# The second attention of a two-layer trunk: a bank of PSUM and a quarter of the probabilities' room for each step of the first tile

## What is computed

```python
SEQ, D_MODEL, CHUNK, Q_BLOCK = 256, 1024, 64, 128
C_HEADS, C_NOPE, C_ROPE, C_V = 16, 64, 32, 64      # C_QK = 96

def mla_mixer(h, ...):
    z = h @ w_in                                   # then two low-rank norms
    q = (c_q @ w_uq).reshape(B, S, C_HEADS, C_QK)
    kv = (c_kv @ w_ukv).reshape(B, S, C_HEADS, C_NOPE + C_V)
    ...                                            # k = nope part and shared rotary part; q, k: rms_norm, rope
    out = dense_chunk_causal_attention(q, k, v, C_QK ** -0.5)
    return out.reshape(B, S, C_OUT) @ w_out

def dense_chunk_causal_attention(q, k, v, scale):  # blocks of 128 queries
    s = jnp.einsum('bqhd,bkhd->bhqk', qb, k) * scale
    p = masked_softmax(s, chunk_causal_mask(b, seq))   # keys of the query's chunk of 64 and before
    return jnp.einsum('bhqk,bkhd->bqhd', p, v)

x = x + mla_mixer(...)
x = x + moe_swiglu(rms_norm(x, l1_norm_ffn), w_router, w_gu, w_down)   # 8 experts, weights of 3584
```

## Time and profile before

| what | value |
|---|---|
| time, median of 3 runs | 1240.6 us (1240.0 to 1243.81) |
| time of the profiled execution | 1238.79 us |
| its span in the trace | 1236.9 us |
| second attention, from the first scores to the last values | 353 to 395 us of the span |
| TensorE busy over the span | 1205.4 us |
| mean granted clock of TensorE | 0.998 |

### The profile page before, as it was taken

One profiled execution on the slowest core, in us unless ns is written; L12 is line 12 of the kernel. 1 busy time (PEld: TensorE's weight loads), 2 busy tenths in 40 slices (PEclk: granted clock), 3 DMA queues, 4 the chain that ended last, 5 costly groups with the idle time before them and its releaser, 6 DMA issues.

```text
span 1236.9 us, 21712 instructions
## 1 busy us (share of the span) xinstructions
PE 1205.4 (97%) x9410; PEld 595.8 (48%) x9410; DVE 530.0 (43%) x1085; ACT 336.2 (27%) x654; POOL 54.4 (4%) x69
## 2 busy tenths in 40 slices
PE   9989999999988999999999999999999999999997
PEld 7757888888777723332433333334333333333332
DVE  6976665556677421232332142133233123314323
ACT  7375555454766300110220020012010011001101
POOL 3300000000430000000000000000000000000000
PEclk9999999999999999999999999999999999999999
DMA  9504545553614999999999999999999999999995
GB/s 370 192 3 145 197 174 186 187 198 113 248 67 193 377 379 405 404 368 430 424 430 425 428 429 426 427 426 386 430 425 426 429 426 429 428 425 427 425 429 240
DMA packets 40277, 413.60 MB, mean 334 GB/s; under 512 B 4720, under 2 KB 5360, under 8 KB 9840
## 3 DMA queue, kind: packets, MB, share of 16 engines
q1 hardware_dynamic: 39888, 412.06, 81.1%
q10 hardware_dynamic: 288, 0.09, 0.0%
HBM read 411.08 MB, written 1.05 MB: 333 GB/s over the span
## 4 chain that ended last, share of the span: by engine, by line
PE 85%; DVE 5%; DMA 3%; ACT 3%; issue 1%; POOL 1%; SPq 0%; DVEq 0%; ACTq 0%; POOLq 0%
PE PS L2530 40%; PE PS L2540 19%; PE PS L1997 6%; PE PS L1999 6%; PE PS L1998 6%; DMA arena<-in_expert_tiles 3%; PE PS L2403 2%; DVE w_split L1303 1%; PE PS L2065 1%; PE PS L2110 1%; PE PS L2435 1%; ACT arena L899 1%; DMA ring<-in_dense_tiles 1%; PE PS L2018 1%; PE PS L2007 1%
## 5 line engine op out<-in xcount | busy, mean ns | idle before, releaser
L2530 PE MATMUL PS<-homes,arena 128*32 128x512 f32 x3192 | 351.5, 592 | 2.6 <-DVE arena L1891 1.7
L2530 PEld LDWEIGHTS PS<-homes,arena 128*32 128x32 f32 x3192 | 102.9, 110 | 240.6 <-issue 232.6
L1884 DVE SCALAR_TENSOR_TENSOR arena<-arena,PS 64x256 f32<-64x256 f32 x126 | 52.1, 414 | 377.0 <-ACT arena L1239 374.9
L2540 PE MATMUL PS<-homes,arena 128*32 128x512 f32 x1896 | 208.8, 592 | 0.0
L1239 ACT ACTIVATE arena<-PS 64x512 f32<-64x512 f32 x63 | 37.2, 590 | 460.5 <-PE PS L2530 460.5
L1997 PE MATMUL PS<-w_split,hT_hi 128*128 128x512 f32 (+2 forms) x372 | 141.9, 381 | 4.2 <-DVE w_split L1303 2.1
L1999 PE MATMUL PS<-w_split,hT_lo 128*128 128x512 f32 (+2 forms) x372 | 139.3, 374 | 0.0
L1998 PE MATMUL PS<-w_split,hT_hi 128*128 128x512 f32 (+2 forms) x372 | 139.2, 374 | 0.0
L2540 PEld LDWEIGHTS PS<-homes,arena 128*32 128x32 f32 x1896 | 61.2, 110 | 140.1 <-issue 139.4
L2530 PE MATMUL PS<-arena 128*32 128x512 f32 x936 | 103.7, 592 | 0.0
L1303 DVE TENSOR_TENSOR w_split<-ring,w_split 128x1024 fp32r<-128x1024 f32 (+1 forms) x60 | 66.8, 1159 | 32.9 <-ACT w_split L844 32.7
(11 more groups left out here) (226 smaller groups left out, 1036.4 us busy)
## 6 DMA issues: line engine op xcount, KB each, us to landing
homes<-in_expert_tiles SPq DMA_DIRECT2D x109, 2048.0 KB, 20.9
ring<-in_dense_tiles SPq DMA_DIRECT2D x49, 1024.0 KB, 4.8
free_homes<-in_expert_tiles SPq DMA_DIRECT2D x17, 2048.0 KB, 22.3
arena<-in_expert_tiles SPq DMA_DIRECT2D x16, 2048.0 KB, 20.5
homes<-in_expert_tiles SPq DMA_DIRECT2D x24, 1024.0 KB, 19.3
arena<-in_expert_tiles SPq DMA_DIRECT2D x18, 1024.0 KB, 22.2
x_res<-in_expert_tiles SPq DMA_DIRECT2D x4, 1024.0 KB, 13.5
ring<-in_dense_tiles SPq DMA_DIRECT2D x6, 512.0 KB, 5.9
```

The source lines that it names most:

```text
L1884: ins = v.scalar_tensor_tensor(out=act_exp[64 * j:64 * (j + 1), g, :], in0=gate[0:64, g, c], scalar=1.0, in1=PS[0:64, gu_banks[k][g], c], ...
L2530: ins = pe.matmul(PS[GROUP * q:GROUP * (q + 1), gu_banks[k][g], :], xT[:, cc, o + g * GROUP:o + (g + 1) * GROUP], quarter(k_home, q), star ...
L2540: ins = pe.matmul(PS[GROUP * q:GROUP * (q + 1), 3 + g, :], tokens_T(k, c, q // 2, g), quarter(k_home, q), start=k == 0 and c == 0, stop=end)
```

## The change

In the second attention alone:

- Steps 0 to 3 each get a PSUM bank of their own (0, 1, 6, 7), with all four heads' 128 columns in it, and each a quarter of `probs`. The small fields of a step get four places instead of two.
- `shares(kind, i)` says how many steps must be done before step i may write: none for steps 0 to 3, two for step 4, four for step 5. `scores`, `exps` wait by it.
- TensorE multiplies the scores of steps 0 to 3 ahead of `last_heads`, steps 2 and 3 behind the wait for the copies that `last_heads` had. `last_heads` has 8 `keep_clock` matmuls in place of 12, and `FILL["C"]` is (3, 3, 1, 1, 0). The loop multiplies scores from step 4 on.
- VectorE's order becomes front 0, 1, 2, back 0, front 3, back 1, back 2, front 4, and from there as before. ScalarE's order is the same.

```diff
-FILL = {"AB": (9, 3, 3, 3, 7), "C": (3, 3, 3, 3, 1)}
+FILL = {"AB": (9, 3, 3, 3, 7), "C": (3, 3, 1, 1, 0)}
...
+        def scores_of(kind, i):
+
+            nk = P * (i // 4 + 1)
+            if kind == "C" and i < 4:
+                return PS[:, (0, 1, 6, 7)[i], :].rearrange("p (m s n) -> p m s n", m=2, s=2)
+            b = 6 * (i % 2)
+            return PS[:, b:b + 2, :].rearrange("p m (s n) -> p m s n", s=2)[:, :, :, 0:nk]
+
+        def probs_of(kind, i):
+
+            if kind == "C" and i < 4:
+                return arena3[:, 512 * i:512 * (i + 1)].rearrange("p (s m n) -> p s m n", s=2, m=2)
+            return probs[:, i % 2, :, :, 0:P * (i // 4 + 1)]
+
+        def shares(kind, i):
+
+            if kind == "C" and i < 6:
+                return 0 if i < 4 else 2 * i - 6
+            return max(i - 1, 0)
...
@@ ScalarE, exps @@
-                    if i >= 2:
-                        a.wait_ge(probs_transposed, s0 + 2 * i - 2)
+                    if shares(kind, i):
+                        a.wait_ge(probs_transposed, s0 + 2 * shares(kind, i))
                         if kind == "C":
-                            a.wait_ge(probs_summed, i - 1)
+                            a.wait_ge(probs_summed, shares(kind, i))
...
@@ VectorE @@
                 front(0)
                 front(1)
+                if kind == "C":
+                    front(2)
                 for j in range(8):
                     back(j)
-                    if j + 2 < 8:
+                    if kind == "C" and j < 2:
+                        if j == 0:
+                            front(3)
+                    elif j + 2 < 8:
                         front(j + 2)
...
@@ TensorE, scores @@
-                    if i >= 2:
-                        pe.wait_ge(exp_done, s0 + 2 * i - 2)
+                    if shares(kind, i):
+                        pe.wait_ge(exp_done, s0 + 2 * shares(kind, i))
...
@@ TensorE, attention @@
                 scores(0)
-                if between is not None:
+                scores(1)
+                if kind == "C":
+                    pe.wait_ge(qkT_ready, 13)
+                    pe.wait_ge(qkT_copied, 7)
+                    scores(2)
+                    scores(3)
                     between()
-                scores(1)
-                if between is not None:
 
                     pe.wait_ge(qkT_ready, 17)
                 for i in range(8):
 
                     if i < len(FILL[kind]):
                         keep_clock(2, FILL[kind][i])
-                    if i + 2 < 8:
+                    if i + 2 < 8 and (kind == "AB" or i > 1):
                         scores(i + 2)
...
             def last_heads():
 
-                keep_clock(6, 12)
+                keep_clock(2, 8)
                 pe.wait_ge(qk_normed, 8)
-                pe.wait_ge(qkT_ready, 13)
-                pe.wait_ge(qkT_copied, 7)
                 transpose_heads1(q1[1], 2)
```

More of the change, by code:

```diff
@@ L407, in build @@
         slot_of = arena[:, 8416:8456].rearrange("p (b e) -> p b e", b=SPLIT_BLOCKS)
-        small = misc[:, 128:192].rearrange("p (k n) -> p k n", k=2)
+        small = {"AB": misc[:, 128:192].rearrange("p (k n) -> p k n", k=2),
+                 "C": misc[:, 128:192].rearrange("p (k n) -> p k n", k=4)}
         k_rope = arena[:, 992:1128].rearrange("p (t n) -> p t n", t=NT)
@@ L887, in exps @@
                     a.wait_ge(bias_ready, s0 // 2 + i + 1)
-                    if i >= 2:
-                        a.wait_ge(probs_transposed, s0 + 2 * i - 2)
+                    if shares(kind, i):
+                        a.wait_ge(probs_transposed, s0 + 2 * shares(kind, i))
                         if kind == "C":
-                            a.wait_ge(probs_summed, i - 1)
-                    sm = small[:, i % 2, :]
+                            a.wait_ge(probs_summed, shares(kind, i))
+                    sm = small[kind][:, i % (2 if kind == "AB" else 4), :]
                     if kind == "AB" and j >= 2:
@@ L898, in exps @@
                             o, c = 2 * m + s, 4 * j + 2 * s + m
[L899 to L900 removed]
+                            ins = a.activation(probs_of(kind, i)[:, s, m, :], scores_of(kind, i)[:, m, s, :], ACT.Exp,
                                                bias=sm[:, 4 + o:5 + o], scale=q_scale[:, 0, t, c:c + 1],
@@ L1372, in front @@
                     nk = P * (t + 1)
-                    b = 6 * (i % 2)
-                    sc = PS[:, b:b + 2, :].rearrange("p m (s n) -> p m s n", s=2)
-                    fields = small[:, i % 2, :].rearrange("p (f m s) -> p f m s", m=2, s=2)
+                    sc = scores_of(kind, i)
+                    fields = small[kind][:, i % (2 if kind == "AB" else 4), :].rearrange("p (f m s) -> p f m s", m=2, s=2)
                     scale = q_scale[:, 1, t, 4 * j:4 * j + 4].rearrange("p (s m) -> p m s", s=2)
@@ L1407, in back @@
                     if kind == "C":
-                        v.tensor_reduce(fields[:, 2], probs[:, i % 2, :, :, 0:nk].rearrange("p s m n -> p m s n"),
+                        v.tensor_reduce(fields[:, 2], probs_of(kind, i).rearrange("p s m n -> p m s n"),
                                         AX.X, ALU.add).then_inc(probs_summed, 1)
@@ L2064, in scores @@
                                 kk = kT1[0:C_QK, 2 * p + m, 0:nk]
-                            ins = pe.matmul(bank(6 * (i % 2) + m)[:, s * SEQ:s * SEQ + nk], q, kk, start=True, stop=True)
+                            ins = pe.matmul(scores_of(kind, i)[:, m, s, :], q, kk, start=True, stop=True)
                     ins.then_inc(scored, 1)
@@ L2082, in transposes @@
                             ins = pe.transpose(bank(2 + i % 2)[:, j * P:(j + 1) * P],
-                                               probs[:, i // 2 % 2, i % 2, m, b * P:(b + 1) * P], ident[:, :])
+                                               probs_of(kind, i // 2)[:, i % 2, m, b * P:(b + 1) * P], ident[:, :])
                     ins.then_inc(probs_transposed, 1)
```

## The result

The changed kernel takes 1248.24 us (median of 4 runs, 1247.87 to 1250.23) against 1240.76 for the kernel before (4 runs, 1240.0 to 1243.81). The ratio is 1.0064, with a 95% interval of 1.0048 to 1.0080: it is slower by 7.5 us. It had the direction but less than half of the size.

A forecast was written before the change was run, and what follows sets the result against it. TensorE was taken as the bound, with attention's delay passed on to the full expert stage. Order +1.9 us and one clock fall +1.3 made +3.2 on the 1240.6 median: 1243.8 us, range 1240.8 to 1246.2.

The forecast's parts named there:

- The order, +1.9: Second attention at full clock: later second-tile transposes delay ScalarE's list, the loop regains some; scores 5 start 1.9 us late.
- lower bound: For the order term, +1.4 us, if scores 2 and the clock matmuls interleave better with their neighbours at three seams.
- The loop's terms: First values to scores 4 gets 1.4 us shorter, to 3.7; scores 4 to scores 5 gets 0.5 shorter, to 3.8.
- The clock, +1.3: One fall of TensorE's granted clock about when the values start, behind a thin stretch, costing 1.3 us (bounds 0 to 2.8).
- the sentence on the top: Ahead of scores 2: dropping the clock matmuls in TensorE's wait for VectorE's copy, 355.2 to 356.55, costs nothing by itself.
- the gap of 1.63 ahead of 380.51 to 1.9: Ahead of step 4's values, in a rival: TensorE's gap stretches by 0.3 us; a further low stretch costs 1.4 us.
- The clock falls more than once: Rival, chance 0.19: further low stretches in the loop or at 382 to 386 us, 1.4 us each; 1245.3 us.
- its 1246.7 for a third stretch: Same rival's time in us if the clock has a third low stretch, each further one priced at 1.4 us.
- The stage behind takes it up: Rival, chance 0.10: expert weights' arrival sets the start of the expert stage, so the delay vanishes; 1240.6 us.
- It is faster: Rival, chance 0.08: heads' transposes aren't late for ScalarE and only the loop's removals count; down to 1237.2 us.

The follow-up runs named there:

- every gap covered: Changed kernel plus clock matmuls: twelve ahead of scores 2, five ahead of the first values, eight ahead of step 4's values; 1242.21 us, ratio 1.0012.
- the version with the heads first: Changed kernel with twelve clock matmuls in the wait, second query tile's transposes ahead of scores 2 and 3, without the eight clock matmuls; 1240.25 us.
- last gap: Changed kernel with eight clock matmuls between the transposes and the values of step 4, nothing else; 1246.62 us, ratio 1.0041.
- last and middle gap together: Changed kernel with five clock matmuls ahead of the first values and eight ahead of step 4's values; 1244.04 us, ratio 1.0028.
- The first gap covered alone, the one with cover at the top: Changed kernel with twelve clock matmuls put into TensorE's wait ahead of scores 2, nothing else; 1247.1 us, ratio 1.0058.
- the faster version: Changed kernel, second query tile's transposes ahead of scores 2 and 3, twelve clock matmuls for the eight, eight ahead of step 4's values; 1238.25 us.
- the kernel before without its twelve: Kernel before the change without its twelve clock matmuls behind scores 0, nothing else; 1242.5 us, ratio 1.0011.
- a leaner loop: Version with heads first and cover ahead of step 4's values, loop clock matmuls cut from (3, 3, 1, 1, 0) to (3, 0, 0, 0, 0); 1237.0 us.

## Why the prediction was wrong

The profiled execution began this attention 0.54 us late (VectorE's last copy at 356.41, not 355.87), and the sums below count that by itself.

**The order, +1.9: the mechanism was right, the size came out at its lower bound.** With every gap covered the changed order costs 2.1 us by the medians, with an interval from nothing to 3 us. The trace of that version shows the terms at full clock. The first values come at 367.29 instead of 362.89, 4.4 us late; less the 1.1 by which the cover overran that is 3.2 or 3.3, where 3.8 was forecast. From scores 2 to the heads' transposes it takes 3.64 us, not 1.9 + 2.0: the length of a run counts an overlap with the next one. The loop's terms hold: 371.06 - 367.29 = 3.77 (forecast 3.7) and 374.88 - 371.06 = 3.82 (forecast 3.8). In all that is 3.2 - 1.4 - 0.5, or +1.4 before rounding, the lower bound of the prediction. In the trace after, scores 4 to scores 5 took 378.78 - 374.97 = 3.81 us too, and first values to scores 4 took 374.97 - 369.89 = 5.08, which is 3.77 and 1.3 for a low stretch. That the delay comes by ScalarE's list agrees with the version with the heads first: its scores 5 start 2.3 us earlier than before (370.71 against 372.30, its copy 0.68 late), where 1.9 was worked out.

**The clock, +1.3: the mechanism was right, the size was not.** The low stretch that was forecast came where it was forecast, behind the first values, at its price. The step that failed is the sentence on the top: "The clock matmuls that covered this gap are gone, which costs nothing by itself." TensorE then had 3.01 us without work ahead of scores 2, longer than any gap in this attention before the change, and the stretch behind it ran at half clock for 6.8 us: from 357.23 to 364.12, 6.9 us, stand scores 2 and 3 and the eight matmuls that were forecast at 3.9. The prediction had worked the gap out as 1.4 us (355.2 to 356.55), because it timed scores 0 and 1 by an execution in which the transposes ahead of them ran at the low clock, 3.37 us; in the kernel after these took 1.95, the scores ended earlier, and the gap was wider. The low clock at that place goes from execution to execution, so this part is chance. The step that failed is not: without the eight clock matmuls the gap was 1.49 us, and the clock fell behind it too. The prediction had looked for thin places in the loop and not at this one.

**The place ahead of step 4's values** was in the text only as part of a rival: "the gap of 1.63 ahead of 380.51 to 1.9", price 1.4. It came as 1.86 us, and the stretch behind it lasted 6.8 us. From the values of step 4 to the first expert transfer went 394.14 - 386.98 = 7.16 us in place of 384.71 - 380.51 = 4.20, so 3.0 and not 1.4. So the rival "The clock falls more than once" is what happened, and even its 1246.7 for a third stretch was too low, since each was priced like the one of 3.4 us at 350 us, and two of the three lasted 6.8.

The sum over the profiled execution, each low stretch taken against the version with every gap covered: 0.5 (began late) + 1.4 (order) + 3.2 (top: 6.89 us from scores 2 to the heads' transposes, not 3.64) + 1.3 (behind the first values) + 3.0 (step 4's values) = 9.4; the transfer was 9.43 late. Over medians the pieces measured by cover are: last gap 1.6, last and middle gap together 4.2, all three 6.0, and 2.1 left, against 8.1 in all by these medians (1248.24 less the 1240.1 of the kernel before beside them). The first gap covered alone gave 1.1, the last alone 1.6 where its stretch in the trace cost 3.0: a median mixes executions in which the clock fell at a place and ones in which it didn't, and the 2.1 left has in it what the cover overran.

**The stage behind takes it up: fell**, with a transfer 9.43 us late and a span 9.7 longer. **It is faster: fell.** That the heads' transposes could come early for ScalarE was excluded in the prediction, and is in fact what the faster version had to do by its order.

The Trainium skill's section "A second HAM failure mode: psum-queue depth-cycling" (page "TensorE: Matmul & The Clock Gate"), weighed in the prediction, says of another kernel, one in bf16, that frequent short idles make the clock swing. The trace after agrees with it: three falls behind gaps of 3.01, 1.21 and 1.86 us. The prediction gave it too small a chance.

**Open:** why some low stretches last 3.4 us and others 6.8, and why the same gap is sometimes survived. The gap of 1.86 us ahead of step 4's values had 3.4 us behind it in the version with heads first, 6.8 in the changed kernel and in the one with cover at the top, and none in the one without the eight clock matmuls. And the longest gap, 3.91 us in the kernel before without its twelve, had a short one. No run was made to part them.

## What to carry to other kernels

Matmuls that fill a wait aren't free to drop: ask what the granted clock does behind each gap that an edit opens, and work out the gap with the engine at full clock, since a stretch that was slow in the profile hides how long the wait is. When work is moved ahead of a wait, put first what other engines are queued behind (here the heads' transposes, for ScalarE's copies), and use the moved work itself as cover behind it: the same scores, one place later, with the waits covered and the eight clock matmuls gone, made of 7.5 us lost a version 1.8 us faster than before, and 3.3 with a leaner loop. How much of that gain a leaner loop would have brought the kernel before, without the new banks, no run shows. And when such a kernel's time spreads over several us from run to run, compare medians over ten runs, not one profile: one execution shows which gaps can be hit, not how often.

## What the hardware showed that was not expected

- A gap of 1.21 or 1.22 us ahead of the first values was enough for the clock to fall, in all five traces that have it (370.8 us in the kernel after). The gap ahead of step 4's values went either way: at 1.63 us the clock stayed high in two traces, the kernel before among them, and fell in one, and at 1.86 us it fell in three and stayed high in one. The length of a gap alone does not tell.
- Every low stretch of this attention in the thirteen traces lasted 3.4 or 6.8 us. TensorE was fully busy inside some of the long ones (6.00 of 6 us from 388 to 394 in the kernel after), so the clock did not come back as soon as there was work.
- The gap of 1.96 us ahead of the first query tile's transposes is the same in all thirteen kernels profiled. In five of these executions a low stretch lay behind it and the transposes took 3.0 to 3.6 us (the kernel before: 3.37); in eight, the kernel after among them, they took 1.95: the same code, the same gap, either outcome.
- Seven of the thirteen executions had a low stretch between 73 and 106 us, in layer 0, which no version touches. In these seven this attention began 0.5 to 2.2 us later than in the kernel before (by VectorE's last copy), in the other six within 0.3 us of it.
